# Where the weight sums of a Strassen FFN are made, and in which order ScalarE empties PSUM

## What is computed

```python
def _conv_ffn(h, w_gu, conv_w, conv_b, w_down):
    g, u = jnp.split(h @ w_gu, 2, axis=-1)
    L = g.shape[1]
    pad = CONV_W // 2
    gp = jnp.pad(g, ((0, 0), (pad, pad), (0, 0)))
    gc = conv_b
    for t in range(CONV_W):
        gc = gc + gp[:, t:t + L] * conv_w[t]
    return (jax.nn.silu(gc) * u) @ w_down
```

## Time and profile before

| | us |
|---|---|
| median of three runs | 3197.89 (3193.79 to 3198.98) |
| the profiled execution | 3194.57 |
| its span, first to last instruction | 3192.8 |
| PE busy | 2902.6 (91% of the span) |
| DVE busy | 2005.9 (63%) |
| ACT busy | 1281.3 (40%) |
| POOL busy | 818.0 (26%) |

### The profile page before, as it was taken

One profiled execution on the slowest core, in us unless ns is written; L12 is line 12 of the kernel. 1 busy time (PEld: TensorE's weight loads), 2 busy tenths in 40 slices (PEclk: granted clock), 3 DMA queues, 4 the chain that ended last, 5 costly groups with the idle time before them and its releaser, 6 DMA issues. The chain is left out here.

```text
span 3192.8 us, 50797 instructions
## 1 busy us (share of the span) xinstructions
PE 2902.6 (91%) x17132; PEld 2553.3 (80%) x17132; DVE 2005.9 (63%) x3113; ACT 1281.3 (40%) x2746; POOL 818.0 (26%) x793
## 2 busy tenths in 40 slices
PE   4899999797999997998699988999899979999997
PEld 0799999545888886886699988998899978888875
DVE  3433432444989895677877788777877753543545
ACT  3111111114878885232455554554555542121121
POOL 0000000111322221222544445444444410302302
PEclk7999999898999998999799999999999989999999
DMA  7322221567346443454332323332233334333333
GB/s 244 98 83 91 84 89 63 207 210 196 86 105 139 99 95 94 150 183 140 98 91 90 95 86 118 100 93 89 78 95 101 90 113 145 117 125 113 117 118 135
DMA packets 358739, 372.29 MB, mean 117 GB/s; under 512 B 87686, under 2 KB 288789, under 8 KB 355893
## 3 DMA queue, kind: packets, MB, share of 16 engines
q1 hardware_dynamic: 339865, 360.86, 37.4%
q10 hardware_dynamic: 18720, 9.44, 1.0%
HBM read 271.10 MB, written 101.12 MB: 117 GB/s over the span
## 5 line engine op out<-in xcount | busy, mean ns | idle before, releaser
L1929 PE MATMUL fu_alpha<-fu_h,fu_w 128*128 128x384 f32 x3168 | 601.1, 342 | 82.7 <-ACT fu_u L2007 64.9
L1929 PEld LDWEIGHTS fu_alpha<-fu_h,fu_w 128*128 128x128 f32 x3168 | 561.2, 192 | 103.7 <-issue 45.4
L2390 PE MATMUL fd_acc<-fd_w,fd_f 128*128 128x512 f32 x2376 | 546.2, 392 | 26.0 <-DVE fd_w L2418 16.6
L2390 PEld LDWEIGHTS fd_acc<-fd_w,fd_f 128*128 128x128 f32 x2376 | 447.3, 189 | 124.8 <-issue 17.6
L1929 PE MATMUL fu_beta<-fu_h,fu_w 128*128 128x384 f32 x1584 | 287.3, 336 | 5.2 <-DVE fu_h L2130 5.2
L1929 PEld LDWEIGHTS fu_beta<-fu_h,fu_w 128*128 128x128 f32 x1584 | 277.3, 189 | 5.6 <-issue 5.6
L517 PE MATMUL pj_gps<-pj_ht,w_in 128*128 128x256 f32 x2160 | 268.1, 284 | 0.0
L2414 DVE TENSOR_TENSOR fd_f<-fd_f_stage,fd_f 128x512 fp32r<-128x512 f32 (+1 forms) x110 | 89.0, 810 | 284.3 <-ACT fd_f L2370 284.3
L517 PEld LDWEIGHTS pj_gps<-pj_ht,w_in 128*128 128x128 f32 x2160 | 262.7, 192 | 1.3
L2126 DVE TENSOR_TENSOR fu_w<-up_w_stage,fu_w 128x512 fp32r<-128x512 f32 x264 | 229.1, 869 | 43.9 <-ACT fu_w L1989 43.9
L2161 DVE SCALAR_TENSOR_TENSOR fu_result<-fu_g,fu_conv_w,fu_result 128x768 f32<-128x768 f32 (+1 forms) x132 | 212.1, 1607 | 61.7 <-ACT fu_result L2029 61.6
(11 more groups left out here) (199 smaller groups left out, 4794.8 us busy)
## 6 DMA issues: line engine op xcount, KB each, us to landing
up_w_stage<-in_w_gu_dram SPq DMA_DIRECT2D x132, 512.0 KB, 5.0
fd_w_stage<-in_w_down_dram SPq DMA_DIRECT2D x54, 512.0 KB, 3.6
fd_f_stage<-f_t SPq DMA_DIRECT2D x88, 256.0 KB, 2.7
at_k<-k_t SPq DMA_DIRECT2D x28, 704.0 KB, 12.7
fo_w<-in_w_ada_dram SPq DMA_DIRECT2D x8, 2048.0 KB, 8.7
ada_w_in_stage<-in_w_in_dram SPq DMA_DIRECT2D x48, 192.0 KB, 3.2
pj_x<-in_x_all_dram SPq DMA_DIRECT2D x9, 1024.0 KB, 4.9
mx_y<-y_mixed SPq DMA_DIRECT2D x18, 512.0 KB, 4.9
```

The lines of the kernel that those rows point to most:

```text
L1929: mm = pe.matmul(out, w[x][:, j, k, :], b[y][:, j, k, :], start=opens and (k, x, y) == (0, HI, HI), stop=(k, x, y) == (KH - 1, LO, HI), sk ...
L2390: mm = pe.matmul(acc[:, t, at], f[a][:, slot, t * P:(t + 1) * P], w[b][:, w_at(st, slot), at], start=is_step(st, 0) and (a, b) == (HI, HI) ...
```

## The change

DVE makes the four weight sums, and only in the first span (22 steps): three of them behind the remainder for A11 (`first_weight_sums`), the last behind that for S4 (`last_weight_sum`). SP's queue stores each, 256 KB, to a new DRAM tensor `w_sums`, and DVE's next sum into the same tile waits for that store. In the other two spans nothing is summed: SP fetches the four stored sums (256 KB each) into the places where they were made, and three quarters of the raw weights (`load_kept_w`, 512 and 256 KB). POOL keeps only the sums of hidden blocks; those of the second and third span it makes in 16 pieces of 384 columns, one behind c11 of each of the steps 2 to 17. `copy_u3` moves from the front of ACT's next step into the step itself, ahead of `silu`; `add_c22` on DVE likewise, ahead of `gate`. `ubuf` gets two buffers.

The diff, cut to its core (renamed arguments and the semaphores' declarations are left out):

```diff
+    def load_kept_w(self, eng, f, slot):
+        eng.dma_start(self.wst[:, slot, 0], self.w_cols[f]).then_inc(self.w_staged[slot], 16)
+        eng.dma_start(self.wst[:, slot, 1, self.KH:KT, :], self.w_cols[FT + f][:, self.KH:KT, :]).then_inc(self.w_staged[slot], 16)
...
-        ubuf = sb("fu_u", [P, SPAN])
+        ubuf = sb("fu_u", [P, 2, SPAN])
...
+                    sp.wait_ge(made, m * 4 + (1, 2, 3, 4)[i])
+                    sp.dma_start(w_sums[f * 4 + i], src.rearrange("p k c -> p (k c)")).then_inc(sum_stored[i], 16)
+
+                def bring_sum(f, i, at):
+                    sp.dma_start(sums[:, at].rearrange("p k c -> p (k c)"), w_sums[f * 4 + i]).then_inc(sum_loaded[at], 16)
+
...
                         sp.wait_ge(w_lo, w_count(n, A22))
-                        sp.wait_ge(made, n * 4 + 4)
-                        up.load_w(sp, f + 2 if not isinstance(f, int) else (f + 2) % FT, par)
+                        if p == 0:
+                            sp.wait_ge(sum_stored[2], n * 16 + 16)
+                            sp.wait_ge(made, n * 4 + 4)
+                        if lp == 0:
+                            up.load_w(sp, lf, par)
+                        else:
+                            up.load_kept_w(sp, lf, par)
+                            sp.dma_start(up.wst[:, par, 1, 0:KH, :].rearrange("p k c -> p (k c)"), w_sums[lf * 4 + 2]).then_inc(s3_loaded[par], 16)
+                            if fixed(n, FT - 2):
+                                keep_sum(m, mf, 0, sums[:, 0])
+                                sp.wait_ge(sum_stored[0], 16 * FT)
+                            sp.wait_ge(w_lo, w_ready(l - 1, S1))
+                            bring_sum(lf, 0, 0)
+                    if mp == 0:
+                        if not fixed(n, FT - 2):
+                            keep_sum(m, mf, 0, sums[:, 0])
+                        keep_sum(m, mf, 1, sums[:, 1])
+                        keep_sum(m, mf, 2, up.wst[:, 1 - par, 1, 0:KH, :])
+                        keep_sum(m, mf, 3, sums[:, 2])
+                    elif mp < SPANS:
+                        if fixed(n, FT - 1):
+                            for i in (2, 3):
+                                sp.wait_ge(sum_stored[i], 16 * FT)
+                        sp.wait_ge(w_lo, w_ready(n, S4))
+                        bring_sum(mf, 3, 2)
+                    if 0 < lp < SPANS:
+                        if fixed(n, FT - 2):
+                            sp.wait_ge(sum_stored[1], 16 * FT)
+                        sp.wait_ge(w_lo, w_ready(l - 1, S2))
+                        bring_sum(lf, 1, 1)
...
+                keep_sum(0, 0, 0, sums[:, 0])
+                keep_sum(0, 0, 1, sums[:, 1])
+                keep_sum(0, 0, 2, up.wst[:, 0, 1, 0:KH, :])
+                keep_sum(0, 0, 3, sums[:, 2])
...
+                def hidden_sum(p, i, out, a, b, made_by):
+
+                    for k in range(KH):
+                        pool.wait_ge(c11_done, p * FT + 3 + i * KH + k)
+                        pool.tensor_tensor(up.hst[:, out, k], up.hst[:, a, k], up.hst[:, b, k], ALU.subtract).then_inc(made_by, 1)
+
+                for p in range(SPANS - 1):
...
+                        pool.wait_ge(up.h_staged[q], (p + 2) * 16)
+                    hidden_sum(p, 0, T1, B12, B11, t12_made)
+                    pool.wait_ge(t12_made, (p + 1) * 8 + 4)
+                    hidden_sum(p, 1, T2, B22, T1, t12_made)
+                    hidden_sum(p, 2, T3, B22, B12, t34_made)
+                    pool.wait_ge(t12_made, (p + 1) * 8 + 8)
+                    hidden_sum(p, 3, T4, B21, T2, t34_made)
...
+                def high_w(m, p, par, j):
+
+                    if j in (S1, S2, S3, S4) and p == 0:
                         act.wait_ge(made, m * 4 + (S1, S2, S3, S4).index(j) + 1)
+                    elif j in (S1, S2, S4):
+                        act.wait_ge(sum_loaded[(S1, S2, S4).index(j)], m * 16 - (FT - 1) * 16)
+                    elif j == S3:
+                        act.wait_ge(s3_loaded[par], (m - par) * 8 - (FT // 2 - 1) * 16)
...
                 def copy_c21(m, p, f, par):
                     act.wait_ge(done[A22], m + 1)
-                    if from_step(m, 1):
-                        act.wait_ge(gated, m)
-                    act.copy(ubuf[:, 0:HALF], alpha[:, par, 0:HALF]).then_inc(c21_done, 1)
+                    if from_step(m, 2):
+                        act.wait_ge(gated, m - 1)
+                    act.copy(ubuf[:, par, 0:HALF], alpha[:, par, 0:HALF]).then_inc(c21_done, 1)
...
-                    if before is not None:
-                        copy_u3(*before)
                     act.wait_ge(done[A11], n + 1)
                     if from_step(n, 1):
                         act.wait_ge(c11_done, n)
                     act.copy(s1[:, :], alpha[:, par, 0:HALF]).then_inc(s1_done, 1)
...
+                    copy_u3(*now)
                     if before is not None:
                         silu(*before)
                         gate_edge(*before)
                     if more:
-                        high_w(n + 1, 1 - par, S3)
+                        high_w(m, mp, 1 - par, S3)
                     if ends:
                         high_b(p + 1, S3)
...
+                def first_weight_sums(m, par):
+
+                    a = [[up.wst[:, par, h, kh * KH:(kh + 1) * KH, :] for kh in range(2)] for h in range(2)]
+                    dve.wait_ge(up.w_staged[par], (m - par) * 16 + 32)
+                    if from_step(m, 1):
+                        dve.wait_ge(w_lo, w_ready(m - 1, S1))
+                        dve.wait_ge(sum_stored[0], m * 16)
+                    dve.tensor_tensor(sums[:, 0], a[1][0], a[1][1], ALU.add).then_inc(made, 1)
+                    dve.wait_ge(made, m * 4 + 1)
+                    if from_step(m, 1):
+                        dve.wait_ge(w_lo, w_ready(m - 1, S2))
+                        dve.wait_ge(sum_stored[1], m * 16)
+                    dve.tensor_tensor(sums[:, 1], sums[:, 0], a[0][0], ALU.subtract).then_inc(made, 1)
+                    dve.tensor_tensor(a[1][0], a[0][0], a[1][0], ALU.subtract).then_inc(made, 1)
+
+                def last_weight_sum(m, par):
+                    dve.wait_ge(made, m * 4 + 2)
+                    if from_step(m, 1):
+                        dve.wait_ge(w_lo, w_ready(m - 1, S4))
+                        dve.wait_ge(sum_stored[3], m * 16)
+                    dve.tensor_tensor(sums[:, 2], up.wst[:, par, 0, KH:KT, :], sums[:, 1], ALU.subtract).then_inc(made, 1)
...
-                    if before is not None:
-                        add_c22(*before)
                     low_next(A11)
+                    if mp == 0:
+                        first_weight_sums(m, 1 - par)
                     low_now(A22)
                     low_next(S1)
                     if before is not None:
                         add_c12(*before)
                     low_now(S4)
+                    if mp == 0:
+                        last_weight_sum(m, 1 - par)
                     if before is not None:
                         later_tap(*before, 1)
...
                     low_next(A12)
+                    add_c22(*now)
                     if before is not None:
                         gate(*before)
                     low_next(S3)
...
-                dve.tensor_tensor(up.hst[:, T1], up.hst[:, B12], up.hst[:, B11], ALU.subtract).then_inc(t12_made, 1)
+                dve.tensor_tensor(up.hst[:, T1], up.hst[:, B12], up.hst[:, B11], ALU.subtract).then_inc(t12_made, 4)
+                first_weight_sums(0, 0)
...
+                dve.wait_ge(t12_made, 4)
+                dve.tensor_tensor(up.hst[:, T2], up.hst[:, B22], up.hst[:, T1], ALU.subtract).then_inc(t12_made, 4)
+                last_weight_sum(0, 0)
...
+    w_sums = scratch("w_gu_sums", [FT * 4, P, KT // 2 * P])
```

More of the change, by code:

```diff
@@ L1789, in ffn_up_phase @@
         stored = [sem(f"fu_stored{s}") for s in range(2)]
+        sum_stored = [sem(f"fu_sum_stored{i}") for i in range(4)]
+        sum_loaded = [sem(f"fu_sum_loaded{i}") for i in range(3)]
+        s3_loaded = [sem(f"fu_s3_loaded{s}") for s in range(2)]
         def every_step(body, end=lambda last: None):
@@ L1824, in ffn_up_phase, with after @@
         width = lambda p: SPAN if p < SPANS - 1 else SPAN + 2
+        def after(n, p, f, by=1):
+            if isinstance(f, int) and f + by >= FT:
+                return n + by, p + 1, f + by - FT
+            return n + by, p, f + by
         def w_source(m, par, j):
@@ L1856, in step @@
                 def step(before, now):
                     n, p, f, par = now
-                    if not isinstance(n, int) or n + 2 < STEPS:
-                        sp.wait_ge(w_lo, w_count(n, A22))
-                        sp.wait_ge(made, n * 4 + 4)
-                        up.load_w(sp, f + 2 if not isinstance(f, int) else (f + 2) % FT, par)
+                    m, mp, mf = after(n, p, f)
+                    l, lp, lf = after(n, p, f, 2)
+                    if fixed(n, FT - 2):
```

(24 more changed lines are left out.)

61 lines of the change are left out of this document (19 added, 42 removed).

## The result

The changed kernel takes 3108.74 us (median of four runs, 3106.93 to 3112.24) against 3195.84 for the kernel before beside it: ratio 0.9728, interval 0.9711 to 0.9745. Two more sets of runs of it gave 3114.25 and 3113.24, ratios 0.9745 (0.9732 to 0.9759) and 0.9743 (0.9728 to 0.9758). The forecast was 3113, range 3098 to 3149.

What follows compares the result with a forecast made beforehand. TensorE was taken to lose time waiting for ACT's u3 copy, 64.9 us in 63 waits. Gains 34 + 34 + 14 + 2 = 84 off 3194.57 gave 3110.6, taken as 3113 for a median; range 3098 to 3149.

Steps and rivals of the forecast that it cites:

- u3 moved, 34 (ordinary steps): Copying u3 in its own step, with add_c22 moved too, ends the 0.71 us lost in each of 48 steps: 34.
- weight sums, 34 (pairs): Weight sums on DVE and quartered POOL hidden sums save 33.7 us in four pairs of steps where POOL sums hidden blocks.
- POOL's pieces: Quarters of POOL's hidden sums behind c11, 1.0 us each in 32 steps, where DVE waits for u3 anyway: no cost.
- Rival 2: POOL's pieces delay a step each by excluding DVE: 32 x 1.0 us, 3145 in all; chance 0.06.
- DMAs: Stores and reloads of sums cost 0: S1's reload has 13.2 us of slack against 2.7 for a 256 KB load.
- rival 3: Late reloads stall S1's rounding, then PE, in 44 steps: 44 us per us beyond 13.2, up to 3368; chance 0.02.
- Ends of spans: Around two span ends, 4 of each 11.1 us lost stays, S3 starting 2.7 late: gain 14 (bounds 4 to 19).
- Start: At the stage's start the first matmul comes about 4 later, given back by step 1's A22: gain 2 (-5 to +6).
- Rivals 1 and 4: 1: a new wait keeps ordinary steps near 15.2, 3153, chance 0.13; 4: copy wrongly blamed, pace stays, 3194, chance 0.03.
- Rival 5: Better than forecast: span ends and start lose almost nothing, 3098; chance 0.06.

Runs made afterwards that it cites:

- Order alone: The kernel before with only u3's copy and add_c22 moved into their own step and two buffers of ubuf: 3128.86 us, ratio 0.9787 to before.
- sums alone: The kernel after with u3's copy and add_c22 back in their old places, the sums' changes kept: 3120.57 us, ratio 0.9762 to before.
- the run's 3370: The kernel after with the reload of S1's sum issued behind A22's remainder of the step that wants it: 3370.05 us, ratio 1.0547 to before.

## Why the prediction was right, and where not

**The sum held**: 84 forecast, 83.2 of span measured. By its parts it is 34, 34, 14.4 and 0.7 of stage, so the mechanism held in the main, with two reasons that were not the right ones (the split of the first two terms, the quarters) and one near hit by luck (the ends):

- **u3 moved, 34 (ordinary steps); weight sums, 34 (pairs).** Both losses are gone, 14.56 in ordinary steps and pairs. But they are not two terms. Order alone and sums alone each remove the 0.71 of the ordinary steps, since a chain that was 0.5 late needs only one cure: a tap 1.02 shorter, or u3 out from behind it. In the pairs the kernel with the sums alone loses nothing, and the order alone takes away some 22 of 33.7. Because the change has both, the sum was right; who had made one half of it would have expected, by this working, at most 34 + 14 + 2 and got 67 or 75.
- **POOL's pieces, 1.0 each, no cost.** The prediction put the end of the pairs' loss down to the quarters; whole sums, one in four steps, lose nothing either, so with the new order it is not the cut that does it. The pieces take 1.38, since each starts beside a remainder of DVE and waits it out (1705.32 and 1705.49 above), and cost nothing. The reason given was right in effect (DVE waits for u3 there) and incomplete: the add that PE waits for is not held by POOL at all. The Trainium skill (SBUF — State Buffer, "SBUF: two separate sides") ties the exclusion to VectorE instructions with two SBUF inputs; the gate's 2.62 and c22's 0.56 beside one POOL sum agree. Rival 2 took every piece to delay a step; the pitch stays 14.56 beside them, and even a whole sum of 3.83 doesn't change it.
- **DMAs, no cost.** A reload took 3.3 us to land in place of the 2.7 assumed, with 13.2 of slack, and a store of a sum 4.9 in place of 2.1; from step 2 of the stage on, no wait of ACT or DVE in it ends with a DMA. The price of rival 3, 44 us per us, left out the clock: with the slack gone each step lost 4.3 waiting and 1.6 in slow matmuls. That the run's 3370 is near the rival's 3368 is chance; its terms were 5.8 and no clock.
- **Ends of spans, 4 left each.** 3.9 are left in the profiled execution, and the walk named the right chain: c12 (line 2206) late behind a hidden remainder (line 2190), then first tap (line 2068), then u2 (the four rows under "The result and the profile after"). Its size was off: 2.7 forecast, of which the prediction made 4 without a source for the other 1.3, and 1.8 measured; the other 2.1 is mostly the clock, which the walk had not priced. Where the clock held, 2.3 was left. So 4 against 3.9 is luck in part.
- **Start, 2.** The first matmul came 9.44 after the stage's entry in place of 6.51, 2.9 later where 4 was forecast; A22 of step 1 51.1 after it in place of 51.8. Gain 0.7.

Rivals 1 and 4 are out by the pitch, rival 2 by the pitch and the whole sums, rival 3 by a landing of 3.3. Rival 5, ends and start that lose almost nothing, is not this kernel, but two buffers for u2 come near it: 3100 against its 3098, with the ends' loss gone and part of the start's. What remains open is which part of the sums' side (POOL free of weight sums, the quarters, their spread over 16 steps) clears the pairs in the old order.

## What to carry to other kernels

When one wait ends a step, list every link ahead of it that can be shortened or stepped around; their gains don't add, and each is priced with the others already in. Ask of a POOL sum which VectorE instructions beside it read two SBUF tiles: here only those waited it out. A wait of 1.8 us on TensorE cost another 1.6 in the matmuls behind it in two executions of three, and waits of 4 did in nearly every step, so a lost margin is priced with the clock at its lower level as well as at the full one.

## What the hardware showed

- The clock behind the same wait is not the program's doing alone: after PE's 1.8 us at the ends of spans 36 matmuls took 8.04 and 8.04, 6.48 and 6.48, 8.06 and 8.08 in three executions of one program. The granted clock around the first of the two waits, from 1875 to 1895 us, was 0.91 in the first and third execution, with a part at 1.2 in place of 2.4 GHz, and 1.00 in the second. What decides it stays open.
- Until the first changed line the executions already differ: the stage was entered at 1524.0 to 1530.8 us over the twelve profiles, which is about the 0.2% that a time can tell.

The two windows of the first point, of the first execution and then of the second, with the columns of the earlier trace rows:

```profile
1875.00:1895.00 20.00, 18.21 (x97) 17.92 (x96) 15.47 (x21) 11.91 (x23) 0.00 (x0) 0.91 0.48 151
```

```profile
1875.00:1895.00 20.00, 18.22 (x106) 17.93 (x105) 17.00 (x23) 13.49 (x26) 0.00 (x0) 1.00 0.51 164
```
